# A float32 block on one core: RMS-norm gain moved into the rounding of the transposed activations, 1/rms into the readers of the products, operands built beside the last chunk

## The chip, the core and the metric

The kernel runs as one program on one core of one Trainium2 chip. The metric is the device time of one execution in microseconds (us), the median over runs. TensorE (PE) multiplies matrices into PSUM, ScalarE (ACT), VectorE (DVE) and GpSimd (POOL) work on elements, SyncE (SP) issues transfers, and ACT and POOL issue some too.

## The reference, cut to what matters

A residual `h` of 256 tokens by 2048 channels, float32, runs through five projections that begin with the same step, the RMS norm:

```python
def _rmsnorm(x, g):
    xf = x.astype(jnp.float32)
    y = xf * lax.rsqrt(jnp.mean(xf * xf, axis=-1, keepdims=True) + EPS)
    return (y * g.astype(jnp.float32)).astype(x.dtype)
...
        a_in = _rmsnorm(h, attn_norm_g[i])
        proj = a_in @ w_in[i]
...
        h = h + jnp.concatenate([y_ssm, y_att], axis=-1) @ w_out[i]
        u = _rmsnorm(h, ffn_norm_g[i]) @ w_up[i]
...
        h = h + (jax.nn.silu(g_ff) * u_ff) @ w_down[i]
        gate = jax.nn.sigmoid(_rmsnorm(h, ple_norm_g[i]) @ w_ple_gate[i])
```

In order they are ATTN (state-space scan and sliding-window attention), FFN (gated feed-forward), PLE (a sigmoid gate), MIX2 (a second block's delta rule and Fourier mixer) and MLP (squared-ReLU feed-forward). Each norm scales a token by one number, 1/rms, and a channel by one number, the gain g; so `norm(h) @ W` equals 1/rms times `(h * g) @ W`.

## The kernel before, in words

**Products.** All weights come as a stream of "quads" of four "slabs" (128 x 1024 float32, 512 KB each), in the order of use. SP loads a slab into `w_raw` as soon as its slot of four is free. ACT rounds it (`split` on ACT: `w_hi`, L704), DVE takes the rest (`split` on DVE: `w_lo = w_raw - w_hi`, L1125), and PE does twelve matmuls of 512 columns per slab (`slab`, L1795 to L1797: high by high, low by high, high by low). Eight slabs make a "chunk": 512 output columns for both tiles of 128 tokens, in a pair of PSUM banks. Pairs 0 and 1 alternate. The left operand, `a_hi` and `a_lo`, is the transposed, rounded activation, in eight pieces of two k-tiles; slab s reads piece s.

**Norm to operand.** After the last chunk of a projection into `h`, DVE adds it (`add_to_h`, L1188), ACT squares it and sums (`squares`, L713), DVE makes the mean (`mean_square`, L1138), POOL takes the power -1/2 (`norm_root`, L505), DVE multiplies `h` by 1/rms and the gain (`normalize`, L1150), a quarter of the channels at a time, PE transposes (`operand_tiles`, L1819, four transposes a piece, into banks 4 to 7), ACT rounds (`rounded_operand`, L733) and DVE takes the rest (`rest_of_operand`, L1131). `first_chunk` puts three pieces ahead of slab 0 and one ahead of each of the slabs 1 to 5. All engines run their instructions in order; semaphores alone tie them.

**POOL.** It also issues the slow loads: the gain row, broadcast to 128 partitions (`load_gain`), ahead of every norm, and two lists of small arrays. The one for MIX2 (`small3_loaded`, seven loads: `s_raw`, `conv2_col` and five masks) stands behind `norm_root(4)` and a wait for the gate's last sum. ACT waits for all seven before it rounds `s_raw`, and only then rounds the weights of MIX2's second chunk.

**Start.** `x` comes in two halves of 1 MB, then the identity, then the first four slabs, then eight small loads, all on SP's queue; POOL loads the first gain row.

Of the kernel before, what the change touches and what calls it, by code (L numbers as in the profile page):

```python
# [77 lines left out]
for _name, _n in (("q_norm_g", HD), ("k_norm_g", HD), ("sinks", HEADS), ("dt_bias", HEADS),  # L78
# [6 lines left out]
GAINS = ("attn_norm_g", "ssm_norm_g", "ffn_norm_g", "ple_post_g", "ple_norm_g",  # L85
         "g_mix_2", "g_mlp_2", "g_final_2")
# [71 lines left out]
NORM_ATTN, NORM_FFN, NORM_PLE, NORM_MIX2, NORM_MLP, NORM_OUT = range(6)  # L158
(G_ATTN, G_SSM, G_FFN, G_POST, G_PLE, G_MIX2, G_MLP, G_OUT) = range(8)
# [24 lines left out]
NORMED = [TT * DC * (k + 1) for k in range(len(GAINS))]  # L184

def program(nc, wstream, small, const, out):

    ctx = ExitStack()
    with ctx:  # L190
# [24 lines left out]
        rstd = sb("rstd", [P, 4])  # L215
# [56 lines left out]
        with ExitStack() as part:  # L272
# [7 lines left out]
            sc = at3("sc", [P, TT, 4 * DNH])  # L280
# [29 lines left out]
            with ExitStack() as inner:  # L310
# [4 lines left out]
                at3b("pad_fr", [P, 16])  # L315
# [18 lines left out]

        narrow_T = sp[0:HEADS, 1:5].rearrange("p m n -> p (m n)")
# [72 lines left out]
        x_loaded = [sem(f"x_loaded{half}") for half in range(2)]  # L408
        small1_loaded = sem("small1_loaded")
        w32_hi_ready, w32_lo_ready = sem("w32_hi_ready"), sem("w32_lo_ready")  # L410
# [5 lines left out]
        dt_mm, dt_t, narrow_copied = sem("dt_mm"), sem("dt_t"), sem("narrow_copied")  # L416
# [4 lines left out]
        back0_evac, back1_evac = sem("back0_evac"), sem("back1_evac")  # L421
# [39 lines left out]
        def _(sp_):  # L461

            for half in range(2):
                cols = slice(half * D // 2, (half + 1) * D // 2)
                sp_.dma_start(h[:, :, cols], small["x_tok"][:, :, cols]).then_inc(x_loaded[half], 16)
            sp_.dma_start(ident[:], const["ident"]).then_inc(x_loaded[1], 16)
            for s in range(QUAD):
                sp_.dma_start(w_raw[:, s, :], wstream[0, s]).then_inc(raw_loaded[s], 16)
# [11 lines left out]

            for c, (done, count) in enumerate(((out_scaled, 1), (out_scaled, 2), (normed, NORMED[G_MLP] + DC), (normed, NORMED[G_MLP] + DC + 1))):
# [6 lines left out]
        def _(pool):  # L488
            step = Chain(pool, pool_step)

            def load_gain(n):

                if n:
                    pool.wait_ge(normed, NORMED[n - 1])
                pool.dma_start(gain[:], small["gains"][n:n + 1, :].to_broadcast([P, D])).then_inc(gain_loaded, 16)
# [130 lines left out]
            load_gain(G_MLP)  # L626
# [66 lines left out]
            norm_root(5)  # L693
            load_gain(G_OUT)
            norm_root(6)
        @block.scalar
        def _(act):
# [21 lines left out]
            def projected_squares(q0, use, junk):  # L719

                for c in range(DC):
# [28 lines left out]
            for half in range(2):  # L750
                act.wait_ge(x_loaded[half], 16 * (half + 1))
                for c in range(half * DC // 2, (half + 1) * DC // 2):
                    squares(h, xs, c)
            split(0, first=True)
            rounded_operand(TR_ATTN, Q_XBC + 1)
            act.wait_ge(small1_loaded, 8 * 16)
            nc.scalar.copy(w32_hi[:], w32_raw[:]).then_inc(w32_hi_ready, 1)
# [1593 lines left out]
```

## Time and profile before

| | us |
|---|---|
| median of 3 runs | 3281.03 (3280.32 to 3283.79) |
| the profiled execution's own time | 3273.69 |
| its span | 3271.9 |
| busy: PE / DVE / ACT / POOL | 3141.9 / 2013.7 / 1381.3 / 310.9 |

The span is what the trace covers; the execution's own time lies 1.8 us above it, and the median 7.3 us above that. Busy times are sums over an engine. PE's mean granted clock is 0.968 of full speed.

### The profile page before, as it was taken

The numbers are of one execution on the slowest core, as the hardware profiler recorded it, in microseconds if no ns is written. First come the engines' busy times: TensorE is split into PE (matmuls) and PEld (weight loads), VectorE is DVE, ScalarE is ACT, GpSimd is POOL, SyncE is SP. The second block draws the span as 40 slices with busy tenths as digits, with TensorE's granted clock in tenths as the row PEclk, the third lists the DMA queues.
The fourth block names the chain that finished last, engine by engine and source line by source line (L and its number), as shares of the span: only waits on it lengthen the run. The fifth ranks groups of instructions, "written<-read, shape, count | busy, mean of one in ns | idle before, by whom it ended". The sixth has DMA issues, their size and how long they took to land.

```text
span 3271.9 us, 43309 instructions
## 1 busy us (share of the span) xinstructions
PE 3141.9 (96%) x14670; PEld 2561.7 (78%) x14670; DVE 2013.7 (62%) x2654; ACT 1381.3 (42%) x1714; POOL 310.9 (10%) x308
## 2 busy tenths in 40 slices
PE   7999999999999999999999989999999999999997
PEld 6888678877888888877788766678877788888886
DVE  5756766556776667765676544445555565656655
ACT  5444444444444444444445311144444444444443
POOL 0004940000000000000000533300000000000000
PEclk9999999999999999999999977799999999999999
DMA  6554333465556555545555100035555555555563
GB/s 217 173 181 154 129 122 129 141 210 176 185 179 197 187 182 178 190 156 177 185 185 168 51 0 0 0 129 193 192 176 177 179 180 193 187 187 185 182 193 130
DMA packets 142119, 518.37 MB, mean 158 GB/s; under 512 B 16160, under 2 KB 16800, under 8 KB 140896
## 3 DMA queue, kind: packets, MB, share of 16 engines
q1 hardware_dynamic: 140016, 504.31, 46.8%
q0 software_dynamic: 1888, 12.56, 1.0%
q8 instruction: 47, 0.77, 0.1%
q10 hardware_dynamic: 144, 0.52, 0.1%
q14 instruction: 24, 0.20, 0.0%
HBM read 515.24 MB, written 2.10 MB: 158 GB/s over the span
## 4 chain that ended last, share of the span: by engine, by line
PE 64%; issue 29%; POOL 3%; DVE 2%; ACT 1%; DMA 0%; DVEq 0%; POOLq 0%; SPq 0%; ACTq 0%
PE bank L1795 18%; PE bank L1796 17%; PE bank L1797 17%; PE bank L2202 1%; PE bank L2159 1%; PE bank L2165 1%; PE bank L1877 1%; PE bank L2201 1%; PE bank L2198 1%; PE bank L2171 1%; PE bank L1819 1%; PE bank L2211 0%; DVE w_lo L1125 0%; PE bank L2137 0%; PE bank L2073 0%
## 5 line engine op out<-in xcount | busy, mean ns | idle before, releaser
L1125 DVE TENSOR_TENSOR w_lo<-w_raw,w_hi 128x1024 fp32r<-128x1024 f32 x952 | 1178.0, 1248 | 863.8 <-ACT w_hi L704 863.6
L704 ACT CAST w_hi<-w_raw 128x1024 fp32r<-128x1024 f32 x952 | 997.5, 1051 | 1370.8 <-PE bank L1797 1322.3
L1795 PE MATMUL bank<-w_hi,a_hi 128*128 128x512 f32 x2816 | 1119.2, 397 | 6.7 <-DVE a_lo L1131 2.9
L1797 PE MATMUL bank<-w_hi,a_lo 128*128 128x512 f32 x2816 | 1100.5, 391 | 0.0
L1796 PE MATMUL bank<-w_lo,a_hi 128*128 128x512 f32 x2816 | 1100.1, 391 | 0.0
L1795 PEld LDWEIGHTS bank<-w_hi,a_hi 128*128 128x128 f32 x2816 | 531.5, 189 | 124.1 <-issue 17.0
L1797 PEld LDWEIGHTS bank<-w_hi,a_lo 128*128 128x128 f32 x2816 | 530.9, 189 | 112.7
L1796 PEld LDWEIGHTS bank<-w_lo,a_hi 128*128 128x128 f32 x2816 | 531.8, 189 | 111.2 <-issue 4.1
L505 POOL TENSOR_TENSOR rstd<-rstd,neg_half 128x2 f32<-128x2 f32 x7 | 5.0, 712 | 2144.8 <-DVE rstd L1139 2144.8
L1795 PE MATMUL bank<-w_hi,m_hi 128*128 128x512 f32 x512 | 202.9, 396 | 5.1 <-DVE m_lo L1743 5.1
L1796 PE MATMUL bank<-w_lo,m_hi 128*128 128x512 f32 x512 | 202.5, 396 | 0.0
L1797 PE MATMUL bank<-w_hi,m_lo 128*128 128x512 f32 x512 | 202.5, 396 | 0.0
L1188 DVE TENSOR_TENSOR h<-h,bank 128x512 f32<-128x512 f32 (+1 forms) x240 | 153.7, 682 | 25.3 <-PE bank L1797 25.3
L1795 PE MATMUL bank<-w_hi,f_hi 128*128 128x512 f32 x352 | 140.9, 400 | 4.7 <-DVE f_lo L1488 4.7
L1796 PE MATMUL bank<-w_lo,f_hi 128*128 128x512 f32 x352 | 139.8, 397 | 0.0
L1797 PE MATMUL bank<-w_hi,f_lo 128*128 128x512 f32 x352 | 139.6, 397 | 0.0
L1795 PEld LDWEIGHTS bank<-w_hi,m_hi 128*128 128x128 f32 x512 | 96.8, 189 | 27.9 <-DVE m_lo L1743 5.4
L1797 PEld LDWEIGHTS bank<-w_hi,m_lo 128*128 128x128 f32 x512 | 96.8, 189 | 22.7
L1796 PEld LDWEIGHTS bank<-w_lo,m_hi 128*128 128x128 f32 x512 | 96.9, 189 | 22.5
L1795 PEld LDWEIGHTS bank<-w_hi,f_hi 128*128 128x128 f32 x352 | 66.9, 190 | 20.7 <-DVE f_lo L1488 5.6
L733 ACT CAST a_hi<-bank 128x512 fp32r<-128x512 f32 x64 | 36.5, 590 | 101.3 <-PE bank L1819 101.2
L1797 PEld LDWEIGHTS bank<-w_hi,f_lo 128*128 128x128 f32 x352 | 66.9, 190 | 15.7
(440 smaller groups left out, 2767.7 us busy)
## 6 DMA issues: line engine op xcount, KB each, us to landing
w_raw<-weights SPq DMA_DIRECT2D x952, 512.0 KB, 4.1
gain<-gains POOLq DMA_DIRECT2D x8, 1024.0 KB, 5.7
h<-x_tok SPq DMA_DIRECT2D x2, 1024.0 KB, 8.7
w_proj_sb<-w_proj POOLq DMA_DIRECT2D x1, 2048.0 KB, 9.2
out<-xn_m SPq DMA_DIRECT2D x4, 512.0 KB, 3.3
level_sb<-c_level POOLq DMA_DIRECT2D x1, 768.0 KB, 5.2
dft_t_sb<-c_dft_t ACTq DMA_DIRECT2D x1, 512.0 KB, 3.4
w_raw<-w_dt SPq DMA_DIRECT2D x1, 256.0 KB, 12.6
```

Source lines behind the costliest of these rows:

```text
L704: nc.scalar.copy(w_hi[:, s, :], w_raw[:, s, :]).then_inc(hi_ready, 1)
L733: nc.scalar.copy(a_hi[:, 2 * i:2 * i + 2, :].rearrange("p k s -> p (k s)"), bank[4 + i % 4][:]).then_inc(a_hi_ready, 1)
L1125: V.tensor_tensor(w_lo[:, s, :], w_raw[:, s, :], w_hi[:, s, :].bitcast(F32), ALU.subtract).then_inc(lo_ready, 1)
L1188: V.tensor_tensor(h[:, t, col], h[:, t, col], pair[p][t][:], ALU.add).then_inc(pair_free[p], 1)
L1795: T.matmul(psum[t][:], left_hi[:, ts], wh, start=first, stop=False)
L1796: T.matmul(psum[t][:], left_hi[:, ts], wl, start=False, stop=False)
L1797: last = T.matmul(psum[t][:], left_lo[:, ts], wh, start=False, stop=final)
L1819: last = T.transpose(bank[4 + i % 4][:, k * SEQ + t * P:k * SEQ + (t + 1) * P], src[:, t, (2 * i + k) * P:(2 * i + k + 1) * P], ident[:])
L1877: last = T.transpose(bank[first + ct // 2][:, (ct % 2) * SEQ + t * P:(ct % 2) * SEQ + (t + 1) * P], src[:, t, col0 + ct * P:col0 + (ct + 1 ...
L2159: last = T.matmul(hd.at(3, n), hd.mk[:, t, d], hd.r[:, t, d], start=True, stop=True)
L2165: last = T.matmul(hd.at(2, n), hd.t[:, t, d], hd.zz[:, t, d], start=True, stop=True)
L2171: last = T.matmul(hd.at(0, n), hd.zz[:, t, d], hd.t[:, t, d], start=True, stop=True)
```

## The change

The gain now multiplies while `h` transposed is rounded: there a channel is a partition, so a column of gains (`gain_col`, made once at the start by one transpose) serves as a scale (`gained` on ACT, `gained_rest` on DVE; two instructions of 256 columns where one of 512 stood). 1/rms multiplies where the products are read (`scaled`, and the scale of Silu and Sigmoid). So PE transposes `h` itself, and six of the eight pieces are built between the slabs of the chunk before (`early_chunk`, `early_operand`), each as soon as its slab has been multiplied; the last two follow ahead of slab 3 of the new chunk (`late_chunk`, `late_operand`), and `mean_square` comes after them. This holds at FFN, PLE, MIX2 and MLP. At PLE the early pieces lie between the slabs of the last down-projection. At the start, `x` comes in four pieces, alternating with the first four slabs, ACT issues the loads of the identity and the gains, and five pieces are transposed ahead of slab 0, the fifth out of the third piece of `x`. Five of eight broadcast gain loads go. The diff, cut to its core (renamed semaphores, `scaled` at some 20 places of the same form, unrolled loops left out):

```diff
-            for half in range(2):
-                cols = slice(half * D // 2, (half + 1) * D // 2)
-                sp_.dma_start(h[:, :, cols], small["x_tok"][:, :, cols]).then_inc(x_loaded[half], 16)
-            sp_.dma_start(ident[:], const["ident"]).then_inc(x_loaded[1], 16)
-            for s in range(QUAD):
-                sp_.dma_start(w_raw[:, s, :], wstream[0, s]).then_inc(raw_loaded[s], 16)
+            for c in range(DC):
+                cols = slice(c * NC, (c + 1) * NC)
+                sp_.dma_start(h[:, :, cols], small["x_tok"][:, :, cols]).then_inc(x_loaded[c], 16)
+                sp_.dma_start(w_raw[:, c, :], wstream[0, c]).then_inc(raw_loaded[c], 16)
             for dst, src in ((w32_raw, small["w_dt"]), (ones, const["ones"]), (row, small["row"].to_broadcast([P, N_ROW])),
...
+            load_gain(G_POST)
+            norm_root(N_FFN)
             pool.wait_ge(pair_free[0], 2 * (U_FF + 1))
             pool.wait_ge(pair_free[1], 2 * (U_FF + 1))
             for dst, src in ((ff_col, "ff_col"), (w_proj, "w_proj"), (p_T, "p_T")):
                 pool.dma_start(dst[:], small[src]).then_inc(small2_loaded, 16)
-            load_gain(G_POST)
-            norm_root(2)
-            load_gain(G_PLE)
-            norm_root(3)
-            load_gain(G_MIX2)
-            norm_root(4)
+            norm_root(N_POST)
+            load_gain(G_OUT)
+            norm_root(N_PLE)
+            norm_root(N_MIX2)
             pool.wait_ge(gated, TT * (D // NC))
             for dst, src in ((s_raw, small["w_scal"]), (conv2_col, small["conv2_col"]), (cum, const["cum"]),
                              (rest, const["rest"]), (chunk_ones, const["chunk_ones"]), (level, const["level"])):
                 pool.dma_start(dst[:], src).then_inc(small3_loaded, 16)
...
+            def gained(n, g, i):
+                act.wait_ge(tr_ready, KT // 2 * n + i + 1)
+                for k in range(2):
+                    last = nc.scalar.activation(a_hi[:, 2 * i + k, :], bank[4 + i % 4][:, k * SEQ:(k + 1) * SEQ], ACT.Copy,
+                                                scale=gain_col[:, g, 2 * i + k:2 * i + k + 1])
+                last.then_inc(a_hi_ready, 1)
+            def scaled(dst, psum, n, t):
+                return nc.scalar.activation(dst, psum, ACT.Copy, scale=rstd[:, n, t:t + 1])
+            def root_of(n):
+                act.wait_ge(rstd_ready, 2 * (n + 1))
+            def early_operand(q, n, g, between):
+                for s in range(QUAD):
+                    split(q + 1, s, s + 1)
+                    gained(n, g, s)
+                between()
+                for s in range(QUAD - 1):
+                    split(q + 2, s, s + 1)
+                    if s < 2:
+                        gained(n, g, QUAD + s)
+            def late_operand(q, n, g, between):
+                split(q + 1, 0, 1)
+                between()
+                split(q + 1, 1, 3)
+                gained(n, g, 6)
+                gained(n, g, 7)
+                split(q + 1, 3, QUAD)
+            def projected_operand(q0, use, junk, n, g):
+                for c in range(DC - 1):
                     split(q0 + 2 * c + 1)
                     if c:
                         squares_of_h(junk, use, c - 1)
                     split(q0 + 2 * c + 2)
-                squares_of_h(junk, use, DC - 1)
-            def rounded_operand(n, q=None):
...
-                    if q is not None and i >= 5:
-                        split(q, i - 5, i - 4 if i < KT // 2 - 1 else QUAD)
+                q = q0 + 2 * (DC - 1)
+                early_operand(q, n, g, lambda: squares_of_h(junk, use, DC - 2))
+                split(q + 2, QUAD - 1)
...
+            act.dma_start(gain_rows, small["gains"].rearrange("n (k p) -> (n k) p", p=P)).then_inc(first_loaded, 16)
+            act.wait_ge(gain_t, 1)
+            nc.scalar.copy(gain_col[:].rearrange("p n k -> p (n k)"), bank[3][:, 0:N_COLUMN * KT]).then_inc(gain_ready, 1)
+            act.wait_ge(gain_ready, 1)
+            for s in range(QUAD):
+                gained(TR_ATTN, C_ATTN, s)
+                split(0, s, s + 1, first=True)
+            for s in range(2):
+                gained(TR_ATTN, C_ATTN, QUAD + s)
+                split(Q_XBC + 1, s, s + 1)
+            gained(TR_ATTN, C_ATTN, 6)
+            gained(TR_ATTN, C_ATTN, 7)
+            split(Q_XBC + 1, 2, QUAD)
+            for c in range(DC):
+                act.wait_ge(x_loaded[c], 16)
+                squares(h, xs, c)
             act.wait_ge(small1_loaded, 8 * 16)
-            nc.scalar.copy(w32_hi[:], w32_raw[:]).then_inc(w32_hi_ready, 1)
+            nc.scalar.copy(w32_hi[:], w32_raw[:]).then_inc(narrow_hi_ready, 1)
...
+            late_operand(Q_QKV2, TR_MIX2, C_MIX2, lambda: squares(h, qkv2, DC - 1, gated, TT * DC))
             act.wait_ge(small3_loaded, 7 * 16)
-            nc.scalar.copy(s_hi[:], s_raw[:]).then_inc(s_hi_ready, 1)
+            nc.scalar.copy(s_hi[:], s_raw[:]).then_inc(narrow_hi_ready, 1)
             q = Q_QKV2
...
+            def gained_rest(n, g, i):
+                dve.wait_ge(a_hi_ready, KT // 2 * n + i + 1)
+                for k in range(2):
+                    last = V.scalar_tensor_tensor(a_lo[:, 2 * i + k, :], bank[4 + i % 4][:, k * SEQ:(k + 1) * SEQ],
+                                                  gain_col[:, g, 2 * i + k:2 * i + k + 1], a_hi[:, 2 * i + k, :].bitcast(F32),
+                                                  ALU.mult, ALU.subtract)
+                last.then_inc(a_lo_ready, 1)
...
+            def early_operand(q, n, g):
+                for s in range(QUAD):
+                    split(q + 1, s, s + 1)
+                    gained_rest(n, g, s)
+                for s in range(QUAD - 1):
+                    split(q + 2, s, s + 1)
+                    if s < 2:
+                        gained_rest(n, g, QUAD + s)
+            def late_operand(q, n, g, norm):
+                split(q + 1, 0, 3)
+                gained_rest(n, g, 6)
+                gained_rest(n, g, 7)
+                split(q + 1, 3, QUAD)
+                mean_square(norm)
...
+            def project_into_h(q0, n, g, norm):
+                for c in range(DC):
+                    q = q0 + 2 * c
+                    if c < DC - 1:
                         split(q + 1)
                         split(q + 2, 0, QUAD - 1)
-                        dve.wait_ge(slab_done, QUAD * (q + 2))
-                        add_to_h(par, bass.ds(i * (2 * NC) + par * NC, NC))
-                        split(q + 2, QUAD - 1)
+                    else:
+                        early_operand(q, n, g)
+                    dve.wait_ge(slab_done, QUAD * (q + 2))
+                    add_to_h(c % 2, slice(c * NC, (c + 1) * NC))
+                    split(q + 2, QUAD - 1)
+                late_operand(q0 + 2 * DC, n, g, norm)
...
+            normalize(pe_tok, pe_tok, N_POST, G_POST)
+            for n in range(DC):
+                for s in range(2):
+                    if s:
+                        dve.wait_ge(slab_done, QUAD * (Q_GATE - 2) + 2 * (n + 1))
+                        add_to_h(n % 2, slice(n * NC, (n + 1) * NC))
+                    if n:
+                        gained_rest(TR_PLE, C_PLE, 2 * (n - 1) + s)
+                    split(Q_GATE - 1 + n // 2, 2 * (n % 2) + s, 2 * (n % 2) + s + 1)
+            late_operand(Q_GATE, TR_PLE, C_PLE, N_PLE)
             for n in range(D // NC):
...
+            def early_chunk(n, ready, q, p, use):
+                chunk(q, p, use, a_hi, a_lo, between={i + 1: lambda i=i: operand_tiles(n, h, ready, i) for i in range(6)})
+            def late_chunk(n, ready, q, p, use):
+                def tiles_of(s):
+                    if s == 3:
+                        operand_tiles(n, h, ready, 6)
+                        operand_tiles(n, h, ready, 7)
+                    pe.wait_ge(a_lo_ready, KT // 2 * n + s + 1)
+                chunk(q, p, use, a_hi, a_lo, between={s: lambda s=s: tiles_of(s) for s in range(KT // SLAB_KT)})
...
+            ple_chunk = h_chunk(U_GATE - 2)
...
+            gate_chunk = lambda c: pe.wait_ge(gated, TT * (c + 1))
+            early_chunk(TR_MIX2, gate_chunk, Q_GATE + 2 * (DC - 1), (DC - 1) % 2, U_GATE)
+            pe.wait_ge(sig_ready, TT * (DC - 1))
...
```

On PE, the stretch in which the last chunk of the projection into `h` (banks 2 and 3) ends and FFN's first chunk (banks 0 and 1) begins. Before, the transposes of the normalised `xn_f` stand here together:

```order
L1797 MATMUL bank3<-w_hi,a_lo 128x512
L1819 MATMUL bank4<-ident_sb,xn_f 128x128 [waits normed]
L1819 MATMUL bank4<-ident_sb,xn_f 128x128 x3
L1819 MATMUL bank5<-ident_sb,xn_f 128x128 x4
L1819 MATMUL bank6<-ident_sb,xn_f 128x128 [waits normed]
L1819 MATMUL bank6<-ident_sb,xn_f 128x128 x3
L1795 MATMUL bank0<-w_hi,a_hi 128x512 [waits lo_ready,a_lo_ready,pair_free0]
```

Now the same place goes from product to product, and the last transposes of the six are those of bank 5, two slabs earlier; the rows of the last two pieces come behind slab 2 of the new chunk:

```order
L1870 MATMUL bank3<-w_hi,a_lo 128x512
L1868 MATMUL bank0<-w_hi,a_hi 128x512 [waits lo_ready,a_lo_ready,pair_free0]
...
L1892 MATMUL bank6<-ident_sb,h 128x128 [waits a_lo_ready,pair_free1]
L1892 MATMUL bank6<-ident_sb,h 128x128 x3
L1892 MATMUL bank7<-ident_sb,h 128x128 [waits a_lo_ready]
L1892 MATMUL bank7<-ident_sb,h 128x128 x3
L1868 MATMUL bank0<-w_hi,a_hi 128x512 [waits lo_ready,a_lo_ready]
```

The wait for `normed` has gone from between the chunks; the wait for the last sum (`pair_free1`) stands three slabs later.

On POOL, from the norm of PLE to the loads of MIX2, before:

```order
L505 TENSOR_TENSOR rstd<-rstd,neg_half 128x2 [waits rstd_ready]
L495 DMA gain<-gains 128x2048 [waits normed]
L505 TENSOR_TENSOR rstd<-rstd,neg_half 128x2 [waits rstd_ready]
L624 DMA s_raw<-w_scal 128x512 [waits gated]
L624 DMA conv2_col_sb<-conv2_col 128x120
```

and now:

```order
L499 DMA gain<-gains 128x2048 [waits normed]
L509 TENSOR_TENSOR rstd<-rstd,neg_half 128x2 [waits rstd_ready] x2
L621 DMA s_raw<-w_scal 128x512 [waits gated]
L621 DMA conv2_col_sb<-conv2_col 128x120
L621 DMA cum_sb<-c_cum 128x256
```

The loads still stand behind the two roots, and the second root waits for a mean that DVE now takes later. On ACT, the end of MIX2's operand, before (`raw_loaded` and `slab_done` are the waits of the weights' rounding):

```order
L733 CAST a_hi<-bank7 128x512 [waits tr_ready]
L704 CAST w_hi<-w_raw 128x1024 [waits slab_done,raw_loaded2]
L704 CAST w_hi<-w_raw 128x1024 [waits slab_done,raw_loaded3]
L968 CAST s_hi<-s_raw 128x512 [waits small3_loaded]
L704 CAST w_hi<-w_raw 128x1024 [waits slab_done,raw_loaded0]
```

and now:

```order
L724 ACTIVATE a_hi<-bank7,gain_col_sb 128x256 [waits tr_ready]
L724 ACTIVATE a_hi<-bank7,gain_col_sb 128x256
L699 CAST w_hi<-w_raw 128x1024 [waits slab_done,raw_loaded3]
L1008 CAST s_hi<-s_raw 128x512 [waits small3_loaded]
L699 CAST w_hi<-w_raw 128x1024 [waits slab_done,raw_loaded0]
```

The wait for the seven loads keeps its place ahead of the second chunk's weights.

## Rows read from the trace of the kernel before

**Rows 1.** Waits of PE: engine, line, releaser: us in total, times, longest.

```profile
PE bank L1819 <- DVE xs L1150: 18.2, 1, 18.2
...
PE bank L1819 <- DVE xn_f L1150: 10.2, 2, 5.2
...
PE bank L1819 <- DVE qkv L1150: 7.1, 1, 7.1
...
PE bank L1819 <- DVE xn_m L1150: 5.1, 1, 5.1
```

**Rows 2.** Timeline at FFN's norm: start us, us, instruction, idle before and releaser.

```profile
692.50 1.05 ACT L704 CAST w_hi<-w_raw 128x1024 fp32r<-128x1024 f32 x1 [1.67 <-PE bank L1797]
...
695.22 1.05 ACT L704 CAST w_hi<-w_raw 128x1024 fp32r<-128x1024 f32 x1 [1.67 <-PE bank L1797]
...
697.99 1.29 DVE L1188 TENSOR_TENSOR h<-h,bank 128x512 f32 x2 [0.47 <-PE bank L1797]
...
703.00 2.74 PE L1819 MATMUL bank<-ident_sb,xn_f 128*128 128x128 f32 x12 [5.16 <-DVE xn_f L1150]
...
718.44 0.60 PE L1819 MATMUL bank<-ident_sb,xn_f 128*128 128x128 f32 x4
...
721.65 0.60 PE L1819 MATMUL bank<-ident_sb,xn_f 128*128 128x128 f32 x4
```

**Rows 3.** Windows: stretch, us, busy of each engine, granted clock, DMA share, GB/s.

```profile
703.00:708.00 5.00, 5.00 (x21) 4.43 (x22) 4.59 (x8) 1.76 (x3) 0.12 (x1) 0.66 0.90 280
```

**Rows 4.** Timeline of PE at PLE's and MIX2's norms.

```profile
1482.47 2.82 PE L1819 MATMUL bank<-ident_sb,xn_f 128*128 128x128 f32 x12 [5.08 <-DVE xn_f L1150]
...
1502.20 0.60 PE L1819 MATMUL bank<-ident_sb,xn_f 128*128 128x128 f32 x4
...
1583.85 2.79 PE L1819 MATMUL bank<-ident_sb,qkv 128*128 128x128 f32 x12 [7.10 <-DVE qkv L1150]
...
1602.43 0.60 PE L1819 MATMUL bank<-ident_sb,qkv 128*128 128x128 f32 x4
```

**Rows 5.** The first 30 us: moved bytes in 40 slices, and PE's first rows.

```profile
GB/s 0 0 33 153 202 279 300 295 328 399 431 426 421 415 390 401 432 410 410 415 404 407 377 367 343 183 17 0 0 229 399 71 0 169 377 153 0 339 415 448
18.19 2.82 PE L1819 MATMUL bank<-ident_sb,xs 128*128 128x128 f32 x12 [18.19 <-DVE xs L1150]
21.30 0.76 PE L1795 MATMUL bank<-w_hi,a_hi 128*128 128x512 f32 x1 [0.28 <-DVE a_lo L1131]
```

**Rows 6.** Loads of `x`, tile h: issue rows, and issue to landing.

```profile
L465 SPq DMA_DIRECT2D h<-x_tok x2: 587/620/652, 0.7 to 1.4; - x2
...
DMA to landing us min/median/max: 6.9/8.7/10.6
```

**Rows 7.** Timeline at MIX2's norm on DVE, POOL and ACT.

```profile
1581.10 0.15 DVE L1138 TENSOR_REDUCE rstd<-stat 128x2 f32<-128x8 f32 x1
...
1582.23 0.59 POOL L624 DMA_DIRECT2D s_raw<-w_scal  x1
...
1585.44 0.54 POOL L625 DMA_DIRECT2D dft_d_sb<-c_dft_d  x1
...
1605.45 0.61 ACT L968 CAST s_hi<-s_raw 128x512 fp32r<-128x512 f32 x1
```

**Rows 8.** Tile dft_d_sb, the last of the seven loads.

```profile
DMA to landing us min/median/max: 7.0/7.0/7.0
```

**Rows 9.** PE after the wait ahead of the last down-projection.

```profile
1452.59 0.80 PE L1795 MATMUL bank<-w_hi,f_hi 128*128 128x512 f32 x1 [4.72 <-DVE f_lo L1488]
...
1457.70 0.39 PE L1795 MATMUL bank<-w_hi,f_hi 128*128 128x512 f32 x1
```

**Rows 10.** Groups by line: count, busy us, mean ns of one, idle before.

```profile
L1125 DVE TENSOR_TENSOR w_lo<-w_raw,w_hi 128x1024 fp32r<-128x1024 f32 x952 | 1178.0, 1248 | 863.8 <-ACT w_hi L704 863.6
...
L733 ACT CAST a_hi<-bank 128x512 fp32r<-128x512 f32 x64 | 36.5, 590 | 101.3 <-PE bank L1819 101.2
...
L1216 DVE SCALAR_TENSOR_TENSOR f_cv<-bank,ff_col_sb,f_cv 128x254 f32<-128x254 f32 (+1 forms) x176 | 72.7, 476 | 6.0 <-DVE f_cv L1210 1.5
```

More of the change, by code:

```diff
@@ L407, in program @@
         pair_free = [sem(f"pair_free{p}") for p in range(4)]
-        x_loaded = [sem(f"x_loaded{half}") for half in range(2)]
+        x_loaded = [sem(f"x_loaded{c}") for c in range(DC)]
         small1_loaded = sem("small1_loaded")
-        w32_hi_ready, w32_lo_ready = sem("w32_hi_ready"), sem("w32_lo_ready")
+        first_loaded, gain_t, gain_ready = sem("first_loaded"), sem("gain_t"), sem("gain_ready")
+        narrow_hi_ready, narrow_lo_ready = sem("narrow_hi_ready"), sem("narrow_lo_ready")
         gain_loaded = sem("gain_loaded")
@@ L747, in pairs_empty @@
                 act.wait_ge(pair_free[1], 2 * (uses + 1))
[L750 to L755, printed above, removed]
+            act.dma_start(ident[:], const["ident"]).then_inc(first_loaded, 16)
+            act.dma_start(gain_rows, small["gains"].rearrange("n (k p) -> (n k) p", p=P)).then_inc(first_loaded, 16)
[14 more added lines that the diff above has]
+                squares(h, xs, c)
             act.wait_ge(small1_loaded, 8 * 16)
-            nc.scalar.copy(w32_hi[:], w32_raw[:]).then_inc(w32_hi_ready, 1)
+            nc.scalar.copy(w32_hi[:], w32_raw[:]).then_inc(narrow_hi_ready, 1)
             q = Q_XBC
@@ L911, in _ @@
             split(q + 2)
+            root_of(N_FFN)
             ff_evac(0, q)
@@ L994, in _ @@
             sc_view = bank[5][:, SEQ:SEQ + TT * 4 * DNH].rearrange("p (t a) -> p t a", t=TT)
-            nc.scalar.activation(beta[:].rearrange("p t d a -> p t (d a)"), sc_view[:, :, 0:2 * DNH], ACT.Sigmoid).then_inc(beta_ready, 1)
+            for t in range(TT):
+                last = nc.scalar.activation(beta[:, t].rearrange("p d a -> p (d a)"), sc_view[:, t, 0:2 * DNH], ACT.Sigmoid,
+                                            scale=rstd[:, N_MIX2, t:t + 1])
+            last.then_inc(beta_ready, 1)
             nc.scalar.activation(aneg2[:], row[:, ROW["a_log_fwd_2"][0]:ROW["a_log_bwd_2"][1]], ACT.Exp).then_inc(aneg_ready, 1)
@@ L1112, in _ @@
                 for t in range(TT):
-                    last = nc.scalar.activation(xn_m[:, t, cols], h[:, t, cols], ACT.Copy, scale=rstd[:, t:t + 1])
+                    last = nc.scalar.activation(xn_m[:, t, cols], h[:, t, cols], ACT.Copy, scale=rstd[:, N_OUT, t:t + 1])
                 last.then_inc(out_scaled, 1)
@@ L1573, in _ @@
             sc_view = bank[5][:, SEQ:SEQ + TT * 4 * DNH].rearrange("p (t a) -> p t a", t=TT)
[L1574 to L1575 removed]
+            for t in range(TT):
+                last = V.scalar_tensor_tensor(sp2[:, 0, t * 2 * DNH:(t + 1) * 2 * DNH], sc_view[:, t, 2 * DNH:], rstd[:, N_MIX2, t:t + 1],
+                                              row[:, ROW["dt_bias_fwd_2"][0]:ROW["dt_bias_bwd_2"][1]], ALU.mult, ALU.add)
+            step(last)
             g2_tok = g2[:].rearrange("p t d a -> p t (d a)")
```

336 lines of the change are left out of this document (166 added, 170 removed).

## The prediction, as it was put on record

> **What bounds the kernel now.** I read the waits first. PE is the bound: it is busy 3141.9 of 3271.9 us, and only its idle time can be saved. Among its waits, those of the transposes (L1819) for the normalised operand stand out: 18.2 us once at the start, 10.2 in two (FFN, PLE), 7.1 once (MIX2), 5.1 once (MLP), 40.6 us in all [rows 1]. These are the places of the change. The timeline shows what a place costs beyond its wait. In steady work a slab takes 2.72 us (ACT's casts, one a slab, start at 692.50 and 695.22); with a transposed piece behind it 3.21 (718.44 to 721.65), so a piece costs 0.49 [rows 2]. At FFN the first transposes start at 703.00 after 5.16 us idle, and the eighth piece starts at 721.65: 18.65 us for five slabs and seven pieces, which cost 5 x 2.72 + 7 x 0.49 = 17.03 in steady work. So 1.62 more are lost: FFN loses 6.8. In this stretch the granted clock is 0.66, part of it at 1.2 instead of 2.4 GHz, after the idle time [rows 3]. PLE, counted the same way: 5.08 + (19.73 - 17.03) = 7.8; MIX2: 7.10 + (18.58 - 17.03) = 8.65 [rows 4]. For MLP I take its wait of 5.1 and FFN's 1.6: 6.7.
>
> **Start.** Slab 0 starts at 21.30 [rows 5]. From there on the rate is nearly steady. What must come first now: `x_loaded[2]`, since the fifth piece stands ahead of slab 0. The two loads of `x` of 1 MB each were issued at 0.7 and 1.4 and landed 6.9 and 10.6 us later, at 7.6 and 12.0, beside POOL's 1 MB of gains [rows 6]. Later the transfers ran at some 0.41 MB/us [rows 5]. The third piece of `x` ends at 2.5 MB of SP's queue (x, weights, x, weights, x, 0.5 MB each): 12.0 + 0.5 / 0.41 = 13.3. Four transposes at the slow clock are a third of 2.82: 0.94 [rows 5]. Slab 0 then starts at 14.3, 7.0 us earlier. One more piece lies ahead of it (0.49 saved behind); against that more of slab 0 is at the slow clock, since fewer transposes run before it: I take 7.0. The first two slabs of weights have landed by then, and ACT and DVE have had the time for them. ACT's eight squares now stand behind the first eight slabs' casts, ahead of the second chunk's; at some 0.59 us each (as a cast of 512 columns [rows 10]) they take 4.7. The second chunk's slabs are not needed until the narrow products of `dt` are done, so I cost the squares at nothing (4.7 if that cover were gone). Bounds: 4 if the shorter rows of the quarters move at half the rate until 12 us; 9 if the third piece is there by 11.5.
>
> **FFN, PLE, MLP.** Between the slabs of the last chunk ACT has a cast and a piece to do (1.05 [rows 2] and between 0.59 and twice that [rows 10]), DVE a `w_lo` and two products of 256 columns, nearest to the convolution's 0.476: 1.25 + 0.95 = 2.20 [rows 10], in a period of 3.21. So both keep up. At PLE half an `add_to_h` (0.64 of 1.29 [rows 2]) comes on top: 2.84, still under 3.21; the add itself must be done within one slab of its last product, and takes 1.29 of 2.72. The last two pieces wait for the last add, which starts 0.3 us after the chunk's end and has 3 slabs, 8.2 us, until PE asks. The mean comes after slab 3 is cast and is wanted at the end of the chunk, ten us later. I find nothing late: the losses go whole, 6.8 + 7.8 + 6.7 = 21.3. The transposes are as many as before. If the 1.6 us each beyond the wait stay for a reason I don't see, 4.8 less.
>
> **MIX2.** Here the stall goes and another comes. Seven loads on POOL stand behind this norm's root, the root behind the mean, and DVE now takes the mean after `split(q+1, 3)`. From the end of the last gate chunk, T = 1583.85 - 7.10 = 1576.75 [rows 4]: slab 3 of the new chunk ends at T + 4 x 2.72 + 2 x 0.49 = 11.9; ACT's cast ends at 13.2 (0.25 for the signal), DVE's `w_lo` at 14.5. From the reduction to the first load's issue there were 1.13 us (1581.10 to 1582.23): T + 15.6, where before it was T + 5.5. The last of the loads was issued 3.2 us after the first and landed 7.0 us later, 10.2 in all [rows 7, 8]. So all have landed at T + 25.8. Queued behind ACT's wait for them are the rounding of `s_raw` and every cast of the second chunk: cast of `s_raw` (0.61, the next starts 0.5 later), cast 1.05, `w_lo` 1.25: T + 28.6. PE asks for that slab at T + 8 x 2.72 + 2 x 0.49 = 22.7. It waits 5.9 us. Before, the loads were long there when ACT came to them at 1605.45 [rows 7]. After a wait of 4.72 us PE took 5.11 us for twelve matmuls instead of 2.72 [rows 9]: 2.4 more. New loss 8.3 for an old one of 8.65: gain 0.35. Bounds: the last load is issued at T + 18.8; if it were there by T + 20, PE would not wait, a gain of 8.65; if the weight stream, which stood still beside them before and now runs, slows them to 12 us, the gain is -1.5. I take the row's 10.2.
> The Trainium skill (DMA: Bandwidth & Descriptors, "Anatomy of one DMA") fits a GpSimd-issued load with 2.0 us plus its bytes at 436 GB/s: for the 1.63 MB of the seven that is an estimate of 5.7 us, against the 10.2 that the trace shows, and by it the total below would be about 3245.
>
> **Evacuations.** Some 50 copies from PSUM become products with a scalar of the same size; PE waits for few of them. I price them at nothing, and 0.3 us if each of three such places costs 0.1.
>
> **Sum.** 7.0 + 21.3 + 0.35 = 28.6 us off the profiled execution's 3273.69, so 3245.1. The median of before is 7.3 us above that execution; against it 3281.0 - 28.5 = 3252.5.
>
> **Rivals.**
> - *The seven loads are hidden after all* (0.20). They land within 6 us of the first issue: T + 21.6, w_lo at T + 24.4, PE waits 1.7 us, keeps its clock, and MIX2 gives 6.95 instead of 0.35: 3246. For it: little else than weights moves then. Against it: the 10.2 us of the rows. The page's estimate above is this case.
> - *The start gives little* (0.13). `x` in short rows, behind weights and beside the gains: if the third piece lands only at 18, slab 0 starts at 19 and 2 us are saved: 3257.5. For it: the rate was low until 5 us [rows 5]. Against it: 0.4 MB/us later.
> - *The pieces don't hide* (0.04, the other side). ACT's and DVE's new halves, 32 pieces' worth, make PE wait in each period. DVE has 3.21 - 2.20 = 1.0 us to spare; for the gain of 28.5 to be eaten each of the 24 early pieces must be 1.2 us late, thus take 4.4 instead of 2.2: a product of 256 columns at 1.6 us instead of 0.476. At 1.8 each piece is 1.65 late, 39.6 in all, and the kernel takes 3292.
> - *Both the first two off and the 1.6's stay* (0.05): 3262, or the change does nothing (waits return as waits for the last add): 3281, which needs an add 8 us late.
>
> **Numbers.** Forecast 0.58, its own range 3247 to 3258. The range of 8 in 10 goes from 3243 (the first rival with a better start) to 3262. What a measurement of this kernel can tell is about 0.2%, 6.6 us. Faster: 0.58 + 0.20 + 0.13 + most of the rest = 0.93; within 0.2%: 0.03; slower: 0.04.
>
> **What would show it.** Right: first slab near 14 us; no idle time of PE over 0.3 us between the last chunk's last matmul and the next chunk's first at FFN, PLE, MLP and MIX2; the mean some 14.5 us after the chunk's end; at MIX2 POOL's first load some 15 us after it and one wait of PE of about 6 us ahead of the second chunk, released by DVE's `w_lo`, its clock down behind it. Wrong: PE waiting in `early_chunk` for `a_lo` or `w_lo`; loads that land within 6 us; waits of the same size elsewhere.

## The result, and the profile after

| | before | after |
|---|---|---|
| median (runs beside each other) | 3280.68 (3273.01 to 3283.79, 4 runs) | 3228.90 (3227.95 to 3231.36, 4 runs) |
| the profiled execution's own time | 3273.69 | 3228.51 |
| its span | 3271.9 | 3226.4 |
| busy: PE / DVE / ACT / POOL | 3141.9 / 2013.7 / 1381.3 / 310.9 | 3122.7 / 1994.7 / 1399.9 / 305.9 |

The ratio is 0.9847 (0.9831 to 0.9862): 51.8 us by the medians, 45.2 by the two profiled executions, where 28.6 were forecast. The predicted 3252.5 lies 23.6 above the measured median; the lower end of the wider range, 3243, lies 14 above it. PE's mean granted clock is 0.969, as before (0.968).

I read the busy row first, since the prediction was about idle time. PE was idle for 130.0 us of the span and is now for 103.7: 26.3 of the 45.5 us by which the span shrank. The other 19.2 are time in which PE was *busy*: in part the low clock behind the stalls, which the forecast counted, but most of it was not in it.

PE's longest waits after (engine, line, releaser: us in total, times, longest):

```profile
PE bank L2247 <- DVE delta_a L1700: 11.6, 4, 3.0
PE bank L2247 <- DVE delta_b L1700: 10.2, 4, 2.8
PE bank L1979 <- DMA work<-gains: 6.6, 1, 6.6
PE bank L1868 <- DVE m_lo L1815: 5.1, 1, 5.1
PE bank L1868 <- DVE w_lo L1170: 4.9, 3, 4.4
PE bank L1868 <- DVE f_lo L1550: 4.7, 1, 4.7
...
PE bank L1892 <- DMA h<-x_tok: 3.0, 1, 3.0
```

The first two, of the delta rule, were 11.4 and 10.2 before; the waits for `m_lo` and `f_lo` were there too. The five waits of [rows 1] are gone. In their place stand the loads at the start (6.6 and 3.0) and one wait for `w_lo` of 4.4 at MIX2. The windows around FFN, from PLE to MIX2 and around MLP (stretch, us, busy of PE, PEld, DVE, ACT, POOL, granted clock, DMA share, GB/s) show that nothing else came:

```profile
665.00:710.00 45.00, 45.00 (x216) 37.31 (x215) 27.29 (x37) 24.50 (x40) 0.52 (x1) 1.00 0.52 176
1438.00:1550.00 112.00, 112.00 (x522) 92.72 (x522) 72.50 (x93) 64.56 (x102) 1.29 (x2) 1.00 0.56 187
2450.00:2510.00 60.00, 60.00 (x282) 49.74 (x281) 34.64 (x43) 30.71 (x50) 0.70 (x1) 1.00 0.54 183
```

PE is busy in every microsecond of them, at a granted clock of 1.00, the 2.4 GHz level, through the last chunk, the boundary and the late pieces.

To see where the time came from, I take events that both programs have and subtract their times. Timeline of PE before:

```profile
174.11 1.97 PE L1877 MATMUL bank<-ident_sb,stage 128*128 128x128 f32 x8 [2.62 <-DVE stage L1297]
...
605.24 1.97 PE L1819 MATMUL bank<-ident_sb,qkv 128*128 128x128 f32 x16 [0.96 <-DVE qkv L1437]
...
755.85 1.39 PE L1877 MATMUL bank<-ident_sb,f_stage 128*128 128x128 f32 x11 [3.14 <-DVE f_stage L1469]
...
1617.02 1.04 PE L1877 MATMUL bank<-ident_sb,s_stage 128*128 128x128 f32 x8
...
2553.49 1.75 PE L1877 MATMUL bank<-ident_sb,m_stage 128*128 128x128 f32 x7 [3.05 <-DVE m_stage L1730]
...
3236.22 0.79 PE L1795 MATMUL bank<-w_hi,m_hi 128*128 128x512 f32 x1 [5.12 <-DVE m_lo L1743]
```

and after (the fourth row answers to 1452.59 of [rows 9]):

```profile
166.38 1.09 PE L1965 MATMUL bank<-ident_sb,stage 128*128 128x128 f32 x8 [2.67 <-DVE stage L1190]
...
599.40 1.97 PE L1892 MATMUL bank<-ident_sb,qkv 128*128 128x128 f32 x16 [0.96 <-DVE qkv L1501]
...
742.56 1.61 PE L1965 MATMUL bank<-ident_sb,f_stage 128*128 128x128 f32 x13 [3.20 <-DVE f_stage L1190]
...
1433.62 0.74 PE L1868 MATMUL bank<-w_hi,f_hi 128*128 128x512 f32 x1 [4.72 <-DVE f_lo L1550]
...
1586.38 1.03 PE L1965 MATMUL bank<-ident_sb,s_stage 128*128 128x128 f32 x8
...
2515.64 1.71 PE L1965 MATMUL bank<-ident_sb,m_stage 128*128 128x128 f32 x7 [3.11 <-DVE m_stage L1190]
...
3189.94 0.80 PE L1868 MATMUL bank<-w_hi,m_hi 128*128 128x512 f32 x1 [5.11 <-DVE m_lo L1815]
```

The differences are 7.7, 5.8, 13.3, 19.0, 30.6, 37.9 and 46.3 us. Stage by stage against the forecast:

| stage | gained | forecast |
|---|---|---|
| start, to the first `stage` | 7.7 | 7.0 |
| rest of ATTN | -1.9 | 0 |
| FFN's norm (to `f_stage`) | 7.5 | 6.8 |
| **FFN's loop (742 to 1433)** | **5.7** | **0** |
| last down-projection, PLE, MIX2 | 11.7 | 7.8 + 0.35 |
| to MLP's first `m_stage` | 7.2 | 6.7 |
| **MLP's loop (2515 to 3190)** | **8.4** | **0** |
| end | -0.8 | 0 |

Two loops gave 14.1 us in which the diff changes only how the products are read out of PSUM, not PE's work. There the matmuls that read `f` or `m` are shorter. Groups by line, of before (count, busy us, mean ns of one, idle before):

```profile
L1795 PE MATMUL bank<-w_hi,m_hi 128*128 128x512 f32 x512 | 202.9, 396 | 5.1 <-DVE m_lo L1743 5.1
...
L1797 PE MATMUL bank<-w_hi,f_lo 128*128 128x512 f32 x352 | 139.6, 397 | 0.0
...
L1797 PE MATMUL bank<-w_hi,a_lo 128*128 128x512 f32 x2816 | 1100.5, 391 | 0.0
```

and of after:

```profile
L1868 PE MATMUL bank<-w_hi,m_hi 128*128 128x512 f32 x512 | 200.4, 391 | 5.1 <-DVE m_lo L1815 5.1
...
L1870 PE MATMUL bank<-w_hi,f_lo 128*128 128x512 f32 x352 | 137.8, 391 | 0.0
```

The matmuls on the other operand (`w_hi,a_lo`) have 391 in both. The timeline of ACT, which casts once a slab, gives the period of a slab there, 2.79 us before:

```profile
2583.46 1.05 ACT L704 CAST w_hi<-w_raw 128x1024 fp32r<-128x1024 f32 x1 [1.74 <-PE bank L1797]
2586.25 1.05 ACT L704 CAST w_hi<-w_raw 128x1024 fp32r<-128x1024 f32 x1 [1.75 <-PE bank L1797]
```

and 2.72 after, as for `a_hi` [rows 2]:

```profile
2545.64 1.05 ACT L699 CAST w_hi<-w_raw 128x1024 fp32r<-128x1024 f32 x1 [1.67 <-PE bank L1870]
2548.36 1.06 ACT L699 CAST w_hi<-w_raw 128x1024 fp32r<-128x1024 f32 x1 [1.67 <-PE bank L1870]
```

Of the 216 slabs that read `f` or `m`, 200 lie in these two loops (the two last down-projections, eight slabs each, lie outside): 14.1 / 200 is 0.07 us a slab, 5.9 ns a matmul.

What else differs for them is where the operands lie. The diff enlarges `rstd` and adds `mean` and `gain_col` ahead of the stage buffers.
### The profile page after: what moved, and what is told of

The parts are those of the page before. It is cut to its first block, busy times and chain, and to the rows that moved or that the text cites. A ratio compares the mean times of both kernels' runs of the same rounds, so it can differ in the third digit from the quotient of the medians.

```text
span 3226.4 us, 43264 instructions
## 1 busy us (share of the span) xinstructions
PE 3122.7 (97%) x14671; PEld 2558.1 (79%) x14671; DVE 1994.7 (62%) x2655; ACT 1399.9 (43%) x1756; POOL 305.9 (9%) x301
## 4 chain that ended last, share of the span: by engine, by line
PE 69%; issue 24%; POOL 3%; DVE 2%; ACT 1%; DMA 1%; DVEq 0%; POOLq 0%; SPq 0%; ACTq 0%
PE bank L1868 19%; PE bank L1870 19%; PE bank L1869 19%; PE bank L2300 1%; PE bank L2257 1%; PE bank L2263 1%; PE bank L2296 1%; PE bank L1965 1%; PE bank L2299 1%; PE bank L2269 1%; PE bank L1892 1%; PE bank L2309 0%; DVE w_lo L1170 0%; PE bank L2118 0%; PE bank L2092 0%
## 5 line engine op out<-in xcount | busy, mean ns | idle before, releaser
L1870 PEld LDWEIGHTS bank<-w_hi,f_lo 128*128 128x128 f32 x352 | 66.5, 189 | 14.1
L1869 PEld LDWEIGHTS bank<-w_lo,f_hi 128*128 128x128 f32 x352 | 66.6, 189 | 13.4
## 6 DMA issues: line engine op xcount, KB each, us to landing
h<-x_tok SPq DMA_DIRECT2D x4, 512.0 KB, 10.2
w_proj_sb<-w_proj POOLq DMA_DIRECT2D x1, 2048.0 KB, 10.2
```

Source lines behind the costliest of these rows:

```text
L1869: T.matmul(psum[t][:], left_hi[:, ts], wl, start=False, stop=False)
L1870: last = T.matmul(psum[t][:], left_lo[:, ts], wh, start=False, stop=final)
```

## The experiments

"Beside" gives the median of the kernel before in runs on the same chip.

### 1 and 2. Only the place of `f` and `m`

```diff
-            at2("pad_part2", [P, 24])
+            at2("pad_part2", [P, 56])
...
-            at4("pad_part4", [P, 24])
+            at4("pad_part4", [P, 56])
```

The same edit on the kernel before brings the operands to plus 128, and on the changed one back to plus 0.

> The kernel before, its two padding tensors 128 bytes longer, so that the down-projections' left operands (f_hi, f_lo, m_hi, m_lo) begin at a multiple of 256 bytes plus 128, as a_hi and w_hi do, instead of at a multiple of 256. Nothing else is changed. Placement theory: their 2592 matmuls fall from 396 to 400 ns to 391 (a slab from 2.79 to 2.72 us), and the kernel gains about 14 us: 3267 by the median, 3260 beside the profiled 3273.7. Rival (the speed-up of these loops comes with the change's own instructions, ACT and DVE reading less beside them): slabs stay at 2.79 and the time at 3281, within 2 us.

> The changed kernel, its two padding tensors 128 bytes longer, so that the same operands begin at a multiple of 256 bytes, as they did before the change. Placement theory: the two loops are slow again, slabs at 2.79 us, and the kernel takes 14 us more than the changed one: 3243, close to what was predicted without this effect (38 us under before by the medians). Rival: 3229, slabs at 2.72.

The kernel before with the edit: 3257.41 beside 3273.49, ratio 0.9958 (0.9943 to 0.9972), 16 us faster. The changed one: 3242.07, 13 us above the changed kernel's 3228.90. Its group, as in the kernel before:

```profile
L1868 PE MATMUL bank<-w_hi,m_hi 128*128 128x512 f32 x512 | 202.9, 396 | 5.1 <-DVE m_lo L1815 5.1
```

In the kernel before with the edit, ACT's casts in MLP's loop:

```profile
2582.96 1.06 ACT L704 CAST w_hi<-w_raw 128x1024 fp32r<-128x1024 f32 x1 [1.67 <-PE bank L1797]
2585.68 1.05 ACT L704 CAST w_hi<-w_raw 128x1024 fp32r<-128x1024 f32 x1 [1.66 <-PE bank L1797]
```

2.72 us, with none of the change's instructions in it. Between the events used above, FFN's loop takes 696.7 us in the kernel before and 691.1 with the edit; in the changed kernel it takes 691.1, and 696.7 with the edit. MLP's loop takes 682.7 and 674.1 in the one, 674.3 and 682.6 in the other. The placement theory holds both ways, and the rival (ACT and DVE reading less) falls. The changed kernel without the luck of its addresses is 31.4 us under the kernel before beside it (ratio 0.9902, 0.9886 to 0.9919), close to the 28.6 of the sum.

### 3 to 5. Which places

Paddings of other sizes, one more between `f_hi` and `f_lo` and between `m_hi` and `m_lo`; in the last kernel one ahead of `w_hi`:

```diff
         with ExitStack() as rings:
+        sb("pad_w", [P, 16])
```

(there, to make room, `pos_i` and `pos_f` share a buffer, as do `mean` and `rstd`, and the stage paddings make up for it).

> The changed kernel with the four operands at other offsets from a multiple of 256 bytes: f_hi 160, f_lo 192, m_hi 224, m_lo 32 (a_hi and w_hi stay at 128). If any distance from 128 costs, all four groups have a mean near 396 ns; if the place within 64 or 128 bytes decides, some stay at 391: f_lo at 192 (a multiple of 64) would be fast, m_hi and m_lo slow. Time between 3229 and 3243.

> As the scan before, other offsets: f_hi 64, f_lo 96, m_hi 128 (as in the changed kernel), m_lo 0. If each operand pays for itself, m_hi's matmuls stay at 391 ns and only m_lo's rise to 396; if the pair of them counts, both rise. f at 64 and 96: slow if the distance from 128 within 256 bytes decides, fast at 64 if a multiple of 64 is enough. Time between 3229 and 3243.

> The changed kernel with everything from the weights' rounded halves on moved up by 64 bytes: w_hi, w_lo, a_hi, a_lo, f, m, fr and y all begin at a multiple of 256 bytes plus 192 instead of plus 128. If the distance between the two operands of a matmul counts (mod 256), nothing changes: slabs at 2.72 us, 3229. If plus 128 as such is the good place, all 11424 matmuls of this kind pay as f_lo and m_lo did off it, 3 to 7 ns each: 34 to 80 us more, 3263 to 3309.

The two scans took 3240.96 and 3240.59, one run each: the offsets off 128 that were tried (32, 64, 96, 160, 192, 224) cost together nearly as much as 0, and a multiple of 64 is not enough. Groups of the second scan, in which `m_hi` is at 128 and `m_lo` at 0:

```profile
L1872 PE MATMUL bank<-w_hi,m_lo 128*128 128x512 f32 x512 | 204.1, 399 | 0.0
L1871 PE MATMUL bank<-w_lo,m_hi 128*128 128x512 f32 x512 | 203.7, 398 | 0.0
L1870 PE MATMUL bank<-w_hi,m_hi 128*128 128x512 f32 x512 | 200.3, 391 | 5.1 <-DVE m_lo L1817 5.1
```

Neither of the two expectations for `m` was quite right: with `m_lo` alone misplaced, its own matmuls are slow (399), and so are those of `w_lo,m_hi` (398), which run just ahead of them while `m_lo` is loaded into PE; `w_hi,m_hi` keeps 391.

The kernel with everything 64 bytes further took 3228.2, a single run, with 391 or 392 ns in the groups of `m` (393 to 399 in the misplaced ones of the scans). So plus 128 is no good place as such; what counts is the distance between buffers modulo 256 bytes, by the groups that pay that of the stationary operand from the moving one, `w_hi` or `w_lo`. That it is the moving one is argued: in every run `w_raw` and `a_hi` begin at the same distance as `w_hi`, and no run moves `w_hi` against them. Modulo 512 isn't needed: in the kernel before with the edit, `f_hi - w_hi` is 126208, 256 more than a multiple of 512, and it is fast.

### 6. MIX2: the seven loads ahead of the root

```diff
-            norm_root(N_MIX2)
             pool.wait_ge(gated, TT * (D // NC))
...
             pool.dma_start(dft_d[:], const["dft_d"]).then_inc(small3_loaded, 16)
+            norm_root(N_MIX2)
```

> The changed kernel with POOL's seven loads for MIX2 ahead of norm_root(N_MIX2) instead of behind it. They then start some 5 us after the gate's last chunk instead of 15 and have landed 9 us later, ahead of ACT's wait. If they are what MIX2 still loses, the wait of 4.43 us and the 2.6 us at the low clock behind it go: 7 us less, 3222. Rival (the loads share the way with the weights of the first MIX2 chunk and delay them, or the root comes late for the readers of the first products): a wait of 1 to 4 us elsewhere in MIX2, 3225 to 3229.

First what the changed kernel did there. Timelines of DVE, POOL, ACT and PE:

```profile
1565.13 0.15 DVE L1198 TENSOR_REDUCE mean<-stat 128x2 f32<-128x8 f32 x1
1566.22 0.58 POOL L621 DMA_DIRECT2D s_raw<-w_scal  x1
1569.42 0.55 POOL L622 DMA_DIRECT2D dft_d_sb<-c_dft_d  x1
1575.25 0.62 ACT L1008 CAST s_hi<-s_raw 128x512 fp32r<-128x512 f32 x1 [11.29 <-DMA dft_d_sb<-c_dft_d]
1578.13 0.80 PE L1868 MATMUL bank<-w_hi,a_hi 128*128 128x512 f32 x1 [4.43 <-DVE w_lo L1170]
1583.41 0.62 PE L1868 MATMUL bank<-w_hi,a_hi 128*128 128x512 f32 x1
```

PE's idle time begins at 1573.70, and the chunk ahead of it takes 8 x 2.72 + 2 x 0.49 = 22.74, so the gate's last chunk ended at T = 1550.96. The mean came at T + 14.2, the first load at T + 15.3, the last had landed at T + 24.3, and PE went on at T + 27.2; the prediction had 14.5, 15.6, 25.8 and 28.6. Behind the wait the granted clock is 0.50, the 1.2 GHz level, for the next twelve matmuls, and they take 5.28 us instead of 2.72.

With the loads ahead, in the timelines of POOL and ACT:

```profile
1553.10 0.58 POOL L620 DMA_DIRECT2D s_raw<-w_scal  x1 [79.27 <-DVE h L1612]
...
1556.31 0.54 POOL L621 DMA_DIRECT2D dft_d_sb<-c_dft_d  x1
...
1564.52 0.62 ACT L1008 CAST s_hi<-s_raw 128x512 fp32r<-128x512 f32 x1 [2.17 <-DMA dft_d_sb<-c_dft_d]
```

ACT still waits for them 2.17 us, under the cover of slabs already rounded, and PE is busy for 49.00 of the 49.00 us from 1543 on. 3221.82 (3220.18 to 3221.88), 7.1 under the changed kernel, as expected; beside 3276.78 the ratio is 0.9838 (0.9822 to 0.9855).

### 7 and 8. The start

```diff
-            load_gain(G_SSM)
...
             norm_root(N_ATTN)
+            load_gain(G_SSM)
```

and for the second kernel SP's order x0 x1 w0 x2 w1 x3 w2 w3 as well.

> The changed kernel with POOL's first load of 1 MB, the gain row of the scan's norm, behind the first norm's root instead of at the very start. If the 1 MB beside x takes the start's bandwidth (the streams moved 0.4 MB/us together), x's second quarter and the first weights come some 2 us earlier and slab 0 starts near 13 instead of 15.2: 3227. If the start is bound by the issue and the latency of x's quarters, slab 0 stays at 15 and the time at 3229.

> As the kernel with the late gain row, and SP's order at the start is x0 x1 w0 x2 w1 x3 w2 w3 instead of x0 w0 x1 w1 x2 w2 x3 w3. x's second quarter then has 1 MB in its queue ahead of its end instead of 1.5, the third 2 instead of 2.5: at 0.4 MB/us 1.2 us each, slab 0 at 12 if bandwidth binds, and no better than the late gain row if latency does. Later slabs must not come late: w3 stands at 4 MB as before.

PE's start in the changed kernel:

```profile
6.85 1.92 PE L1892 MATMUL bank<-ident_sb,h 128*128 128x128 f32 x8
11.74 1.97 PE L1892 MATMUL bank<-ident_sb,h 128*128 128x128 f32 x8 [2.98 <-DMA h<-x_tok]
14.42 1.09 PE L1892 MATMUL bank<-ident_sb,h 128*128 128x128 f32 x4 [0.71 <-issue]
15.16 0.78 PE L1868 MATMUL bank<-w_hi,a_hi 128*128 128x512 f32 x1
```

and with both edits:

```profile
6.33 3.62 PE L1895 MATMUL bank<-ident_sb,h 128*128 128x128 f32 x16
10.58 1.09 PE L1895 MATMUL bank<-ident_sb,h 128*128 128x128 f32 x4 [0.63 <-issue]
11.64 0.77 PE L1871 MATMUL bank<-w_hi,a_hi 128*128 128x512 f32 x1
```

Slab 0 starts at 15.16, 12.71 with the late gain row, and 11.64 with the order too; the times are 3226.53 and 3225.50 (one run each). The wait for `x` of 2.98 us is gone (0.25 is left with the late gain row alone). Slab 0 follows the third quarter of `x`, the last that it needs, by 0.8 to 1.1 us in all three: the quarter landed at 14.3 (issued at 3.49, 10.8 us), 11.9 (3.46, 8.4) and 10.5 (2.71, 7.8). So bytes bound the start, and a gain row of 1 MB that is needed only for the scan's norm took part of them. The differences in time are near what can be measured; slab 0's place in the trace is clear.

### 9. Without the early pieces

```diff
-                chunk(q, p, use, a_hi, a_lo, between={i + 1: lambda i=i: operand_tiles(n, h, ready, i) for i in range(6)})
+                chunk(q, p, use, a_hi, a_lo)
+                for i in range(4):
+                    operand_tiles(n, h, ready, i)
```

with pieces 4 and 5 ahead of slabs 1 and 2 of the next chunk, and ACT and DVE rounding all six behind the last chunk's weights. At FFN, MIX2 and MLP.

> The changed kernel with the gain at the rounding and 1/rms in the readers, but at FFN, MIX2 and MLP none of the six pieces beside the last chunk: four stand between the chunks and two ahead of slabs 1 and 2 (PLE is left as changed). If the early placing earns the gain, each of the three places loses some 4 to 7 us again: 3241 to 3250. If it is enough that the norm is no longer in the way (h's first three quarters are there when the chunk ends, and only transposes, two roundings of 256 columns, 0.84 us, and two rests, 0.87, lie ahead of slab 0), PE waits some 1.5 us and then half a us at a low clock at each place: 3229 + 3 x 1.5 to 2 = 3234.

3235.44 (3234.74 to 3236.11): 6.5 us above the changed kernel. Around MIX2 PE's waits are:

```profile
1553.08 0.47 PE L1862 MATMUL bank<-w_hi,a_hi 128*128 128x512 f32 x1 [0.73 <-DVE a_lo L1181]
1564.07 1.09 PE L1886 MATMUL bank<-ident_sb,h 128*128 128x128 f32 x8 [1.62 <-DVE h L1606]
1585.68 0.80 PE L1862 MATMUL bank<-w_hi,a_hi 128*128 128x512 f32 x1 [6.52 <-DVE w_lo L1167]
```

At FFN the way from `qkv`'s transposes (598.66) to `f_stage` (743.32) is 144.66 us, against 143.16 in the changed kernel: 1.5 of FFN's 7.5 us come from placing the pieces early. The other 6.0 stay with the norm's absence between the chunks.

The three places are not alike. From MIX2's first `s_stage` to MLP's first `m_stage` the kernel lost 1.3 us (1593.32 to 2523.86, against 1586.38 to 2515.64), but from the last down-projection to that `s_stage` 4.5 (1436.08 to 1593.32, against 1433.62 to 1586.38). There the edit moved something else as well: the gate's last add into `h` began 12.3 us after the chunk's end (1562.72) instead of 2.1, the mean came 20.7 us after it (1571.18) instead of 14.2, and so the wait behind the seven loads grew from 4.43 to 6.52. So MIX2's share is not the price of the placing alone.

### 10. The mends together

Edits 6, 7 and 8 in one kernel.

> The changed kernel with the three mends together: POOL's loads for MIX2 ahead of the norm's root (7.1 us by the medians), the late gain row and the order x0 x1 w0 x2 w1 x3 w2 w3 at the start (3.2 us at slab 7 in the trace). They lie at different places and should add: 3228.9 - 10.3 = 3218.6. If the start's gain is lost at a later wait for a transfer or for POOL in the scan, 3221.5.

3216.20 (3214.84 to 3216.89, 5 runs), beside 3273.32, ratio 0.9824 (0.9810 to 0.9838): 12.7 under the changed kernel where 10.3 were expected. It is the fastest of all. Its ATTN behind the start happened to be 1.7 us shorter (161.91 to 593.21, 431.3 us, for the way of 433.0 from 166.38 to 599.40), a variation that is taken up below; and its start is 4.5 us ahead at the first of these events, where 3.2 were expected.

## Why the prediction was wrong, step by step

- **"Only its idle time can be saved"** is the step that failed. But for the low clock behind the stalls it took PE's busy time as fixed, so the sum has no term for PE's time on `f` and `m`. Experiments 1 and 2 show that 13 to 16 us of it hung on the addresses of `f` and `m` against those of the weights, and that the change moved these addresses without a word in its description. The groups of the kernel before already had 396 ns on `m` and 391 on `a_lo`, and the sizes of the new buffers stood in the diff. I took neither for a question.
- **"The median of before is 7.3 us above that execution"**, carried over to the changed kernel, was the second failing step. The changed kernel's median lies 0.4 above its profiled execution. In later sets the kernel before had medians of 3273.3 to 3276.8, with runs from 3270.9 up. With 16.6 us too little in the sum and 7.0 for the offset, the 23.6 are accounted for. Why runs of the kernel before scatter more stays open.
- **Start, 7.0**: 7.7 by the event at 166.38. Slab 0 came at 15.16 instead of 14.3, 6.1 us earlier than in [rows 5]: the third quarter of `x` landed at 14.3, where the sum had 13.3. The rest was made up behind it: the sum says that one more piece lies ahead of slab 0, but there are two (five against three), and by slab 6 the lead was 7.7. It is 7.7 at the first `stage` too, so ACT's squares, priced at nothing, took nothing from it. Right within its bounds.
- **FFN 6.8, PLE 7.8, MLP 6.7**: mechanism right, sizes low. FFN gave 7.5, MLP 7.2; my count ended at the start of the eighth piece and so left out the two slabs behind it. In the kernel before the first of them takes 3.21 us and ends in a wait of 0.20 for `w_lo`, and the second takes 2.84 (to 728.07), 0.6 more than twice 2.72; at PLE, MIX2 and MLP the pair costs the same 0.6:

```profile
722.02 0.47 PE L1795 MATMUL bank<-w_hi,a_hi 128*128 128x512 f32 x1
...
725.23 0.47 PE L1795 MATMUL bank<-w_hi,a_hi 128*128 128x512 f32 x1 [0.20 <-DVE w_lo L1125]
```

For the last down-projection, PLE and MIX2 together 11.7 instead of 8.2. Of the 3.5 more, MIX2's new loss has 1.3 (below), the pairs behind the eighth piece at PLE and at MIX2 0.6 each, the down-projection's first twelve matmuls 0.7 (5.11 in [rows 9], 4.45 after), its other seven slabs 0.5 by their operands' place: 3.7.
- **MIX2 +0.35**: mechanism right, the wait stood where, behind what, and for whom the prediction put it. Sizes: wait 4.43 instead of 5.9, loads 9.0 instead of 10.2, low clock 2.6 instead of 2.4, so a new loss of 7.0 for 8.3, and against the old one of 8.65 a gain of 1.7, or 2.2 with the 0.6 that the count left out of the old one. The prediction is wrong in that the weight stream stood still beside the loads before: from 1582.2 to 1592.6 the DMA moved 245 GB/s, 2.5 MB, of which the seven loads are 1.6. The rival "hidden after all" did not come true. The Trainium skill (DMA: Bandwidth & Descriptors, "Anatomy of one DMA") gave an estimate of 5.7 us for the seven loads; the traces show 9.0 behind the root and, issued earlier, 1553.10 to 1564.51, 11.4, in which the DMA moved 314 GB/s in all against 243. The measurement decides.
- **The pieces hide**: yes, PE is busy for 45 of 45, 112 of 112 and 60 of 60 us. That rival is out. But experiment 9 shows what the sum did not ask: hiding them earns only 1.5 us at FFN and 1.3 at MLP.
- **Evacuations at nothing**: no wait for them was found. ATTN behind the start lost 1.9 us; with the same instructions there, the kernel of experiment 6 took 430.44 us (167.36 to 597.80) for the way that takes 433.02 in the changed kernel and 431.13 in the one before. Behind the same wait of 2.7 us for POOL, 16 small matmuls took 3.68 us in the changed kernel and 2.00 in that of experiment 6. So this is variation between kernels with the same instructions there, in PE's pace behind POOL's waits, and not the change; what sets it stays open.

## What to carry to other kernels

Before you sum what an edit does to the order, list which buffers it moves, and compare the mean time of one instruction of a kind across buffers in the trace of before: a group that is 1% slower than its twins is a question. If a stall is to go, ask first for the smallest step that takes the chain out of the way (here the algebra), and only then for the placing of what is left. And a long list of slow loads belongs ahead of whatever its queue waits for, not behind it.

## What the runs showed of the hardware

A float32 matmul of 512 columns (operands of type fp32r) took 390 to 392 ns by the profile's count (up to 397 in the groups that hold the matmuls behind stalls or pieces) when the stationary operand and the moving one began at the same distance from a multiple of 256 bytes in their partitions, and 393 to 402 when they did not (seven wrong offsets, in four kernels). By slabs it is 2.72 against 2.79 us, 2.5%. Moving all of them by 64 bytes changed nothing. The Trainium skill (TensorE: Matmul & The Clock Gate, "Step-by-step: what each phase is for") says that PE has two independent read ports, so that loading the next weights takes no bandwidth from the running matmul; here, with `m_lo` alone misplaced, the matmul beside which it was loaded rose from 391 to 398 ns, and the one on `m_lo` itself to 399. The first fits a clash of the two reads, which that sentence leaves no room for; the second it does not explain. Nothing here looks at the ports, so the mechanism is open and only the dependence on the addresses is shown.
